# Last expert and final norm of a mixer and mixture-of-experts encoder: four row tiles normed early, two shared between GpSimd and ScalarE, the last products and the expert's own rows by halves

## The chip, the cores and the metric

The kernel runs on one core of one Trainium2 chip. The metric is the device time of one execution in microseconds. The engines are TensorE (PE in the profile; PEld is its weight load), VectorE (DVE), ScalarE (ACT), GpSimd (POOL) and SyncE (SP), which here only issues DMAs.

## The reference, cut to what matters

One encoder layer on 1024 tokens of width 1024, all in float32: a norm, a mixer with two branches, a norm, a mixture of 16 experts in which every expert chooses 128 tokens, and a final norm. The change lies wholly behind the mixer.

```python
# capacity = 2 * 1024 // 16 = 128 tokens for each expert
xg = h[idx]                                       # (16, 128, 1024)
act = silu(xg @ w_gate[e]) * (xg @ w_up[e])       # (128, 2816)
y = (act @ w_down[e]) * gate[e]                   # (128, 1024)
x = x + scatter_add(y, idx)
out = x * rsqrt(mean(x * x, axis=-1) + 1e-6) * norm_final
```

## The kernel before, in words

The function `experts` runs the 16 experts one after the other. `loop` makes a loop of 15 experts and writes the last one out by itself (`last` is true in its body). Each engine has its own instruction list, in a fixed order, and semaphores join them.

**Units.** An expert's weights come in 36 units, numbered k from 0 to 35 (`order`): gate and up products of a tile of 1024, 1024 or 768 hidden columns in four units each (units 0 to 15 and 20 to 27), and down products of the three tiles (units 16 to 19, 28 to 31, 32 to 35). A unit is two blocks of 128 rows; the last two, 34 and 35, have one block each. Float32 precision comes from two parts of each operand: the high part is a rounded copy and the low part the rest, and a product is three matmuls (high by high, high by low, low by high), so that a unit of two blocks is 12 matmuls of 512 (or 384) columns.

**What a unit goes through.** SP loads it into one of nine `raw` buffers as soon as the unit nine before it is split (L1884). ACT makes the high part (`split_high`, L1982), three units ahead of the product and not before the product of the unit four earlier is done, since there are four `part` buffers. DVE makes the low part (`split_low`, L2068), and PE multiplies (L2271 for gate and up, L2245 for down). Between them ACT computes Silu (L2020), DVE the product with `up` (L2132), PE transposes it (L2221), and ACT and DVE split the transposed tile (L2025, L2138). The program lists of ACT and DVE go by steps p from 0 to 35. In step p stand first the Silu, product or transpose work that falls due and then the split of unit k = p + 3, and behind it what `SQUARE_AT`, `MEAN_AT`, `SQRT_AT`, `ROOT_AT` and `NORM_AT` put at that k. The transpose of the third hidden tile stands ahead of unit 30 on PE (`TURN_AT`), its DVE part in step 31, ahead of the splits of units 34 and 35, and unit 32 needs it.

**The end.** The final norm works on eight tiles of 128 tokens. `x_mid` in HBM holds all rows but for what the last expert adds. Tiles 0 and 1 are loaded by POOL during the last expert into `store` and `early_sb`, squared by ACT with a sum for each row (`square_rows`, L2005), and their inverse root comes from DVE and ACT together: `mean_of_rows` (L2111), a square root on ACT (`root`, L2011) and five small operations on DVE (`inverse_root`, L93 to L97). `norm_row` (L2122) multiplies by the root and the gain row, and POOL stores the tile. Tiles 2 to 7 are loaded by SP, two tiles at a time, into raw buffers that have become free (L1900); their squares and norms stand behind the last split on ACT and DVE, and SP stores each behind its norm (L1909). ACT's square root needs another table than Silu, and `act_idle` (L2040) loads it ahead of the end.

The last expert's own rows are not scattered. POOL gathers them from `x_mid` into `xg`, and DVE adds the weighted products (L2178); they are squared, normed (L2186), and written over their rows of the output by an indirect DMA of POOL (L1968). This DMA waits for all stores of the eight tiles (`out_stored`, `early_stored`) and for `own_normed`, since the tiles' stores write stale versions of the same rows. In the order of DVE behind the loop: root and norm of tiles 2 and 3, mean and root of tiles 4 and 5, own rows added, norm of 4 and 5, mean and root of tiles 6, 7 and the own rows together, norm of 6 and 7, norm of the own rows.

The lines that the change touches and the prediction names: `order` and `TURN_AT` (L1758), the tables at L1805 to L1813, SP's loads and stores (L1900, L1909), POOL's part (L1938 to L1968), `square_rows` and `root` (L1997 to L2011), DVE's list behind the loop (L2169 to L2187), and PE's loop over `order` (L2224).

## Time and profile before

| | us |
|---|---|
| median of 3 runs | 2780.15 |
| lowest and highest run | 2779.88, 2780.17 |
| span of the profiled execution, from first to last instruction | 2777.4 |
| PE busy in the span | 2700.3 |
| DVE busy in the span | 1914.0 |
| ACT busy in the span | 1619.2 |
| POOL busy in the span | 221.1 |

The profiled execution has no time of its own beside its span; the median of the runs is 2.75 us above that span, which is what lies around it. Times in the rows are in microseconds from the start of the span, durations marked ns in nanoseconds. In a timeline, a group's first number is its start, the second its length, and brackets tell how long the engine had been idle and who released it. L12 is line 12 of the kernel before. Instructions of DVE and ACT overlap their neighbours by 0.08 to 0.1 us in the records, so a row of DVE costs its list some 0.08 less than its duration. In a group of several instructions the length is that of the whole group.

### The profile page before, as it was taken

The numbers are of one execution on the slowest core, as the hardware profiler recorded it, in microseconds if no ns is written. First come the engines' busy times: TensorE is split into PE (matmuls) and PEld (weight loads), VectorE is DVE, ScalarE is ACT, GpSimd is POOL, SyncE is SP. The second block draws the span as 40 slices with busy tenths as digits, with TensorE's granted clock in tenths as the row PEclk, the third lists the DMA queues.
The fourth block names the chain that finished last, engine by engine and source line by source line (L and its number), as shares of the span: only waits on it lengthen the run. The fifth ranks groups of instructions, "written<-read, shape, count | busy, mean of one in ns | idle before, by whom it ended". The sixth has DMA issues, their size and how long they took to land.

```text
span 2777.4 us, 36831 instructions
## 1 busy us (share of the span) xinstructions
PE 2700.3 (97%) x13530; PEld 2323.1 (84%) x13530; DVE 1914.0 (69%) x1928; ACT 1619.2 (58%) x1483; POOL 221.1 (8%) x242
## 2 busy tenths in 40 slices
PE   8999999999999999948999999999999999999997
PEld 7888888888888888847888888888888888888886
DVE  6624425364554234368889888988888888888887
ACT  6233334353442322326877787777777777877786
POOL 0011010100111111000000000000000000000010
PEclk9999999999999999979999999999999999999998
DMA  4133342421525433358999999999999999999997
GB/s 124 44 104 62 76 89 60 88 76 54 107 56 127 97 93 121 122 220 304 384 381 376 384 383 383 373 387 380 382 379 389 374 386 373 392 373 382 376 392 285
DMA packets 253891, 689.96 MB, mean 248 GB/s; under 512 B 18444, under 2 KB 75916, under 8 KB 253808
## 3 DMA queue, kind: packets, MB, share of 16 engines
q1 hardware_dynamic: 227968, 622.01, 59.9%
q0 software_dynamic: 25840, 66.80, 10.8%
q8 instruction: 58, 0.95, 0.1%
q14 instruction: 25, 0.20, 0.0%
HBM read 634.22 MB, written 54.53 MB: 248 GB/s over the span
## 4 chain that ended last, share of the span: by engine, by line
PE 53%; DVE 2%; issue 0%; DMA 0%; ACT 0%; DVEq 0%; POOL 0%; POOLq 0%; ACTq 0%
PE e_gate_ps L2271 17%; PE e_up_ps L2271 17%; PE e_y_ps L2245 17%; PE e_turn L2221 1%; PE e_turn L2205 1%; DVE e_part L2068 0%; DVE e_top_at L2084 0%; DVE e_top L2080 0%; DVE e_silu L2086 0%; DVE e_act L2086 0%; DMA e_xg<-h_mid,e_token_next 0%; DVE e_raw L2122 0%; DMA out_dram<-e_raw 0%; ACT e_part L1982 0%; DVE e_xg L2178 0%
## 5 line engine op out<-in xcount | busy, mean ns | idle before, releaser
L2068 DVE TENSOR_TENSOR e_part<-e_raw,e_part 128x2048 fp32r<-128x2048 f32 (+2 forms) x576 | 1196.5, 2111 | 176.2 <-ACT e_part L1982 172.9
L1982 ACT ACTIVATE e_part<-e_raw 128x2048 fp32r<-128x2048 f32 (+2 forms) x576 | 1008.7, 1773 | 307.8 <-PE e_y_ps L2245 167.9
L105 PE MATMUL m_proj<-m_hT,m_w_part 128*128 128x512 f32 (+1 forms) x2328 | 548.2, 393 | 1.8 <-ACT m_stage L622 1.8
L105 PEld LDWEIGHTS m_proj<-m_hT,m_w_part 128*128 128x128 f32 (+1 forms) x2328 | 434.3, 187 | 93.6 <-issue 2.2
L2245 PE MATMUL e_y_ps<-e_part,e_actT 128*128 128x512 f32 x2112 | 497.9, 392 | 0.4 <-DVE e_actT L2138 0.4
L2271 PE MATMUL e_gate_ps<-e_part,e_xgT 128*128 128x512 f32 (+1 forms) x2304 | 495.2, 372 | 0.0
L2271 PE MATMUL e_up_ps<-e_part,e_xgT 128*128 128x512 f32 (+1 forms) x2304 | 489.0, 371 | 0.0
L2271 PEld LDWEIGHTS e_gate_ps<-e_part,e_xgT 128*128 128x128 f32 x2304 | 421.9, 188 | 60.8 <-issue 0.3
L2271 PEld LDWEIGHTS e_up_ps<-e_part,e_xgT 128*128 128x128 f32 x2304 | 421.6, 188 | 59.9
L2245 PEld LDWEIGHTS e_y_ps<-e_part,e_actT 128*128 128x128 f32 x2112 | 392.6, 188 | 80.1 <-issue 0.8
L888 DVE TENSOR_TENSOR m_w_part<-m_w_raw,m_w_part 128x1024 fp32r<-128x1024 f32 (+1 forms) x93 | 112.7, 1218 | 142.1 <-ACT m_w_part L546 142.1
L105 PE MATMUL m_out<-m_w_part,m_hT 128*128 128x256 f32 x1536 | 192.5, 283 | 0.0
L105 PEld LDWEIGHTS m_out<-m_w_part,m_hT 128*128 128x128 f32 x1536 | 189.5, 191 | 3.0
L631 ACT ACTIVATE m_lit<-m_proj 128x512 f32<-128x512 f32 x64 | 38.3, 599 | 256.2 <-PE m_proj L105 256.2
L105 PE MATMUL m_proj<-m_oT,m_w_part 128*128 128x512 f32 x768 | 187.3, 394 | 0.2
L105 PEld LDWEIGHTS m_proj<-m_oT,m_w_part 128*128 128x128 f32 x768 | 140.6, 188 | 30.3 <-DVE m_w_part L888 1.6
L622 ACT ACTIVATE m_stage<-m_proj 128x512 f32<-128x512 f32 x128 | 75.9, 597 | 100.7 <-PE m_proj L105 100.7
L1920 POOL TENSOR_TENSOR e_pool_idle<-cst 128x1 f32<-128x1 f32 x30 | 26.3, 876 | 1316.6 <-ACT e_y L2056 1056.2
L546 ACT ACTIVATE m_w_part<-m_w_raw 128x1024 fp32r<-128x1024 f32 (+1 forms) x93 | 96.6, 1051 | 30.6 <-PE m_out L105 12.3
L105 PE MATMUL m_out<-m_w_part,m_mT 128*128 128x512 f32 x384 | 92.1, 394 | 1.8 <-DVE m_w_part L888 1.8
L105 PEld LDWEIGHTS m_out<-m_w_part,m_mT 128*128 128x128 f32 x384 | 70.7, 188 | 17.0 <-DVE m_w_part L888 2.7
L613 ACT ACTIVATE m_v<-m_out 128x512 f32<-128x512 f32 x32 | 19.1, 598 | 110.4 <-PE m_out L105 110.4
(289 smaller groups left out, 1848.4 us busy)
## 6 DMA issues: line engine op xcount, KB each, us to landing
e_raw<-in_w_down_dram SPq DMA_DIRECT2D x160, 1024.0 KB, 7.6
e_raw<-in_w_gate_dram SPq DMA_DIRECT2D x128, 1024.0 KB, 7.3
e_raw<-in_w_up_dram SPq DMA_DIRECT2D x128, 1024.0 KB, 8.6
e_raw<-in_w_gate_dram SPq DMA_DIRECT2D x64, 768.0 KB, 8.8
e_raw<-in_w_up_dram SPq DMA_DIRECT2D x64, 768.0 KB, 5.9
m_w_raw<-in_w_in_dram SPq DMA_DIRECT2D x64, 512.0 KB, 4.5
ret_sum<-m_stage POOLq DMA_DIRECT2D x64, 256.0 KB, 4.7
gla_sum<-m_stage POOLq DMA_DIRECT2D x64, 256.0 KB, 4.7
```

The lines of the kernel that those rows point to most:

```text
L105: last = nc.tensor.matmul(out, x_at(x[xi], kc), w_at(w[wi], kc), start=start and kc == 0 and (xi, wi) == (0, 0), stop=stop and kc == chunk ...
L546: nc.scalar.activation(part_block(n, 0), raw_block(n), ACT.Copy).then_inc(w_high, 1)
L622: proj_took(nc.scalar.activation(stage[:, n % 4], proj_bank(u)[:], ACT.Copy), u)
L631: proj_took(nc.scalar.activation(lit_sb[:, n % 4], proj_bank(u)[:], ACT.Silu if u[0] == "C" else ACT.Sigmoid), u)
L888: nc.vector.tensor_tensor(part_block(n, 1), raw_block(n), part_block(n, 0), ALU.subtract).then_inc(w_split, 1)
L1920: nc.gpsimd.tensor_tensor(pool_idle[:, at:at + 1], cst[:, C_EPS:C_EPS + 1], cst[:, C_EPS:C_EPS + 1], ALU.add).then_inc(carried, 1)
L1982: nc.scalar.activation(part[k % PARTS][0][:, 0:size(k)], raw[k % RAW][:, 0:size(k)], ACT.Copy).then_inc(w_high, 1)
L2068: nc.vector.tensor_tensor(part[k % PARTS][1][:, 0:size(k)], raw[k % RAW][:, 0:size(k)], part[k % PARTS][0][:, 0:size(k)], ALU.subtract).th ...
L2205: last = nc.tensor.transpose(turn[u][:, c, :], xg[:, kc * P:(kc + 1) * P], ident)
L2221: last = nc.tensor.transpose(turn[g][:, c, :], act_sb[:, b * P:(b + 1) * P], ident)
L2245: ins = nc.tensor.matmul(y_ps[:, half, :], actT[i % 2][xi][:, c, :], w[wi][:, j * D + 512 * half:j * D + 512 * half + 512], start=(i, c, x ...
L2271: ins = nc.tensor.matmul(dst[:, half, 0:half_wide], xgT[xi][:, kc, :], w[wi][:, j * wide + half * half_wide:j * wide + (half + 1) * half_w ...
```

## The change

- **Early tiles.** There are three `early` buffers beside `store`, and so tiles 0 to 3 are normed within the last expert. POOL loads tiles 2 and 3 once unit 11 of the last expert is split. Their squares stand on ACT behind the high parts of units 26 and 27, their mean on DVE behind the low part of unit 28, the root on ACT behind unit 29's and on DVE behind unit 30's, and their norms on DVE behind units 32 and 33. POOL stores them. The idle square root (L2040) is gone. SP's list keeps two loads of two tiles (4 and 5, 6 and 7), which wait for units 27 and 28.
- **Squares of tiles 4 and 5** stand on ACT behind the high parts of units 34 and 35. Behind the last split, DVE's list is: mean and root of 4 and 5, norm of 4, mean and root of 6 and 7, left half of the own rows, norm of 5, right half of the own rows, and the own rows' norm.
- **Tiles 6 and 7** are multiplied by the gain row on GpSimd (SBUF to SBUF, 128x1024, into `store` and the first early buffer), behind POOL's stores of tiles 2 and 3; ACT multiplies by the root (`place_row`), and SP stores them last.
- **Last products.** Units 33, 34 and 35 are multiplied first for the left 512 output columns (12 matmuls), which raise `half_done`, and then for the right 512 (12 matmuls). All 24 matmuls are those of before, in another order.
- **Own rows by halves.** Each half is added and squared by itself. Their mean, root and the norm of the left half are on DVE; the right half is multiplied by the gain on DVE into `silu` and by the root on ACT. `own_normed` is raised twice, and POOL's indirect DMA waits for both.

```diff
-        early_sb = sb("early", [P, D])
...
-        X_RAW = [None] + [(UNITS - RAW + m) % RAW for m in range(NT // 2 - 1)]
...
-        early = [store, early_sb]
+        early = [store, *early_sb]
...
+        X_RAW = [None] * (EARLY // 2) + [(UNITS - RAW + m) % RAW for m in range((NT - EARLY) // 2)]
...
-        END_GROUPS = ((0, 2), (2, 4), (4, 6), (6, OWN + 1))
-        SQUARE_AT = {16: 0, 17: 1}
-        MEAN_AT, SQRT_AT, ROOT_AT = 18, 19, 20
-        NORM_AT = {21: 0, 23: 1}
+        GAINED = {6: early[0], 7: early[1]}
+        KEPT = len(GAINED)
+        END_GROUPS = ((0, 2), (2, 4), (4, 6), (6, NT))
+        SQUARE_AT = {16: 0, 17: 1, 26: 2, 27: 3, UNITS - 2: 4, UNITS - 1: 5}
+        MEAN_AT, SQRT_AT, ROOT_AT = {18: 0, 28: 1}, {19: 0, 29: 1}, {20: 0, 30: 1}
+        NORM_AT = {21: 0, 23: 1, 32: 2, 33: 3}
+        FINAL = UNITS - 3
...
-                    for m in range(1, NT // 2):
-                        sp.wait_ge(w_split, UNITS * LAST + UNITS - RAW + m)
+                    for m in range(EARLY // 2, NT // 2):
+                        sp.wait_ge(w_split, UNITS * LAST + UNITS - RAW + m - EARLY // 2 + 1)
...
-                                     ).then_inc(x_in[EARLY + m - 1], 16)
+                                     ).then_inc(x_in[EARLY // 2 + m], 16)
...
-                sp.wait_ge(normed, t + 1)
-                sp.dma_start(out[0, t * P:(t + 1) * P, :], x_tile(t)).then_inc(out_stored, 16)
+                if t in GAINED:
+                    sp.wait_ge(row_placed, t - min(GAINED) + 1)
+                    src = GAINED[t][:]
+                else:
+                    sp.wait_ge(normed, t + 1)
+                    src = x_tile(t)
+                sp.dma_start(out[0, t * P:(t + 1) * P, :], src).then_inc(out_stored, 16)
...
+                        if t == KEPT:
+                            pool.wait_ge(w_split, UNITS * LAST + 12)
...
-                        pool.dma_start(out[0, t * P:(t + 1) * P, :], x_tile(t)).then_inc(early_stored, 16)
+                        pool.dma_start(out[0, t * P:(t + 1) * P, :], x_tile(t)).then_inc(early_stored[t >= KEPT], 16)
+                    pool.wait_ge(gain_in, 16)
+                    pool.wait_ge(early_stored[0], 16 * KEPT)
+                    pool.wait_ge(x_in[EARLY // 2 + min(GAINED) // 2], 16)
+                    for t in GAINED:
+                        nc.gpsimd.tensor_tensor(GAINED[t][:], x_tile(t), gain_row[:], ALU.mult).then_inc(row_gained, 1)
...
-            pool.wait_ge(early_stored, 16 * EARLY)
+            pool.wait_ge(early_stored[0], 16 * KEPT)
+            pool.wait_ge(early_stored[1], 16 * (EARLY - KEPT))
...
-            pool.wait_ge(own_normed, 1)
+            pool.wait_ge(own_normed, 2)
...
-                    act.wait_ge(x_in[t if t < EARLY else EARLY + t // 2 - 1], 16)
-                else:
-                    act.wait_ge(own_added, 1)
+                    act.wait_ge(x_in[t if t < EARLY else EARLY // 2 + t // 2], 16)
...
-                nc.scalar.activation(squares[:], x_tile(t) if t < OWN else xg[:], ACT.Square, accum_out=stat[:, 0, t:t + 1]
+                nc.scalar.activation(squares[:], x_tile(t), ACT.Square, accum_out=stat[:, 0, t:t + 1]
...
+            def square_own(half):
+                act.wait_ge(own_added, half + 1)
+                act.wait_ge(squared, NT + half)
+                nc.scalar.activation(squares[:, 0:D // 2], xg[:, half * (D // 2):(half + 1) * (D // 2)], ACT.Square,
+                                     accum_out=stat[:, 4 * half, OWN:OWN + 1]).then_inc(squared, 1)
+            def place_row(t):
+                act.wait_ge(row_gained, t - min(GAINED) + 1)
+                act.wait_ge(end_rooted, 1)
+                nc.scalar.activation(GAINED[t][:], GAINED[t][:], ACT.Copy, scale=stat[:, 2, t:t + 1]
+                                     ).then_inc(row_placed, 1)
...
-                    if last and k == SQRT_AT:
-                        root(0)
-                    if last and k == UNITS - 2:
-                        nc.scalar.activation(act_idle[:], cst[:, C_EPS:C_EPS + 1], ACT.Sqrt)
+                    if last and k in SQRT_AT:
+                        root(SQRT_AT[k])
...
-                    square_rows(2)
-                    square_rows(3)
-                    root(1)
-                    square_rows(4)
-                    square_rows(5)
...
-                    for t in range(6, OWN + 1):
-                        square_rows(t)
+                    square_rows(6)
+                    square_rows(7)
...
+                    place_row(6)
+                    square_own(0)
+                    place_row(7)
+                    square_own(1)
+                    act.wait_ge(meaned, len(END_GROUPS) + 1)
+                    nc.scalar.activation(stat[:, 1, OWN:OWN + 1], stat[:, 3, OWN:OWN + 1], ACT.Sqrt).then_inc(rooted, 1)
+                    act.wait_ge(own_gained, 1)
+                    act.wait_ge(end_rooted, 2)
+                    nc.scalar.activation(xg[:, D // 2:D], silu[:, 0:D // 2], ACT.Copy, scale=stat[:, 2, OWN:OWN + 1]
+                                         ).then_inc(own_normed, 1)
...
-                    if last and k == MEAN_AT:
-                        mean_of_rows(0)
-                    if last and k == ROOT_AT:
-                        root_of_rows(0)
+                    if last and k in MEAN_AT:
+                        mean_of_rows(MEAN_AT[k])
+                    if last and k in ROOT_AT:
+                        root_of_rows(ROOT_AT[k])
...
-            mean_of_rows(1)
-            root_of_rows(1)
-            norm_row(2)
-            norm_row(3)
+            def add_own(half):
+                at = slice(half * (D // 2), (half + 1) * (D // 2))
+                nc.vector.scalar_tensor_tensor(out=xg[:, at], in0=y_ps[:, half, :], scalar=weight[:, LAST:LAST + 1],
+                                               in1=xg[:, at], op0=ALU.mult, op1=ALU.add).then_inc(own_added, 1)
...
-            dve.wait_ge(gathered, 16 * EXPERTS + 16)
-            dve.wait_ge(unit_done, PARTS + UNITS * EXPERTS)
-            halves = xg[:].rearrange("p (h n) -> p h n", h=2)
-            nc.vector.scalar_tensor_tensor(out=halves, in0=y_ps[:], scalar=weight[:, LAST:LAST + 1], in1=halves,
-                                           op0=ALU.mult, op1=ALU.add).then_inc(own_added, 1)
...
-            norm_row(5)
...
-            norm_row(6)
-            norm_row(7)
-            nc.vector.scalar_tensor_tensor(out=xg[:], in0=xg[:], scalar=stat[:, 2, OWN:OWN + 1], in1=gain_row[:],
-                                           op0=ALU.mult, op1=ALU.mult).then_inc(own_normed, 1)
+            dve.sem_inc(end_rooted, 1)
+            dve.wait_ge(gathered, 16 * EXPERTS + 16)
+            dve.wait_ge(half_done, 1)
+            add_own(0)
+            norm_row(5)
+            dve.wait_ge(unit_done, PARTS + UNITS * EXPERTS)
+            add_own(1)
+            dve.wait_ge(own_added, 2)
+            nc.vector.tensor_tensor(silu[:, 0:D // 2], xg[:, D // 2:D], gain_row[:, D // 2:D], ALU.mult
+                                    ).then_inc(own_gained, 1)
+            own = lambda r: stat[:, r, OWN:OWN + 1]
+            dve.wait_ge(squared, NT + 1)
+            chain.link(nc.vector.tensor_scalar(own(2), own(0), 1.0 / D, EPS, ALU.mult, ALU.add))
+            dve.wait_ge(squared, NT + 2)
+            nc.vector.scalar_tensor_tensor(out=own(3), in0=own(4), scalar=1.0 / D, in1=own(2), op0=ALU.mult, op1=ALU.add
+                                           ).then_inc(meaned, 1)
+            dve.wait_ge(rooted, len(END_GROUPS) + 1)
+            inverse_root(nc, chain, own(2), own(1), own(3), own(4))
+            dve.sem_inc(end_rooted, 1)
+            nc.vector.scalar_tensor_tensor(out=xg[:, 0:D // 2], in0=xg[:, 0:D // 2], scalar=own(2),
+                                           in1=gain_row[:, 0:D // 2], op0=ALU.mult, op1=ALU.mult
+                                           ).then_inc(own_normed, 1)
...
+            def finish(e):
+                for half in range(2):
+                    for k in range(FINAL, UNITS):
+                        _, i, c0, n = order[k]
+                        pe.wait_ge(w_split, UNITS * e + k + 1)
+                        for j in range(n):
+                            c = c0 + j
+                            for xi, wi in ((0, 0), (0, 1), (1, 0)):
+                                ins = nc.tensor.matmul(
+                                    y_ps[:, half, :], actT[i % 2][xi][:, c, :],
+                                    part[k % PARTS][wi][:, j * D + 512 * half:j * D + 512 * half + 512],
+                                    start=False, stop=(c, xi, wi) == (BLOCKS[TILES - 1] - 1, 1, 0))
+                    if half:
+                        ins.then_inc(unit_done, UNITS - FINAL)
+                    else:
+                        ins.then_inc(half_done, 1)
...
+                    if last and k == FINAL:
+                        finish(e)
+                        break
```

## Rows read from the trace of the kernel before

**Rows 1.** First part of the page: busy time, share of the span and instructions.

```profile
PE 2700.3 (97%) x13530; PEld 2323.1 (84%) x13530; DVE 1914.0 (69%) x1928; ACT 1619.2 (58%) x1483; POOL 221.1 (8%) x242
```

**Rows 2.** The chain that ended last, its end; start us, us, what.

```profile
2750.88 8.44 PE e_y_ps L2245 x36
...
2759.44 1.28 DVE e_xg L2178
...
2766.98 2.71 DMA out_dram<-e_raw
...
2770.49 1.01 POOL out_dram L1968
```

**Rows 3.** Timeline of PE, units 32 to 35; brackets: idle before, and releaser.

```profile
2750.88 8.43 PE L2245 MATMUL e_y_ps<-e_part,e_actT 128*128 128x512 f32 x36 [0.42 <-DVE e_actT L2138]
```

**Rows 4.** Timeline of DVE, from the split of unit 27 on.

```profile
2733.83 8.50 DVE L2068 TENSOR_TENSOR e_part<-e_raw,e_part 128x1536 fp32r<-128x1536 f32 x4 [1.74 <-ACT e_part L1982]
2742.24 0.95 DVE L2132 TENSOR_TENSOR e_act<-e_silu,e_up_ps 128x768 f32<-128x768 f32 x1
2743.11 6.69 DVE L2068 TENSOR_TENSOR e_part<-e_raw,e_part 128x2048 fp32r<-128x2048 f32 x3
2749.72 1.01 DVE L2138 TENSOR_TENSOR e_actT<-e_turn,e_actT 128x512 fp32r<-128x512 f32 x2
2750.65 2.35 DVE L2068 TENSOR_TENSOR e_part<-e_raw,e_part 128x1024 fp32r<-128x1024 f32 x2
...
2754.37 0.17 DVE L93 RECIPROCAL e_stat<-e_stat 128x2 f32<-128x2 f32 x1 [0.27 <-ACT e_stat L2011]
...
2755.37 2.48 DVE L2122 SCALAR_TENSOR_TENSOR e_raw<-e_raw,e_stat,e_y 128x1024 f32<-128x1024 f32 x2
```

**Rows 5.** Timeline of ACT, from the split of unit 26 on.

```profile
2728.80 1.49 ACT L1982 ACTIVATE e_part<-e_raw 128x1536 fp32r<-128x1536 f32 x1 [0.87 <-PE e_gate_ps L2271]
2730.31 1.28 ACT L2020 ACT_TABLE_LOAD   x1
...
2732.31 8.70 ACT L1982 ACTIVATE e_part<-e_raw 128x1536 fp32r<-128x1536 f32 x5
```

**Rows 6.** Groups by form, 2700 to 2777 us; name, count | busy us, mean ns | idle.

```profile
L2138 DVE TENSOR_TENSOR e_actT<-e_turn,e_actT 128x512 fp32r<-128x512 f32 x3 | 2.0, 682 | 0.0
...
L2005 ACT ACTIVATE e_squares<-e_raw 128x1024 f32<-128x1024 f32 x6 | 6.3, 1056 | 0.3
```

**Rows 7.** GpSimd's only multiplications or additions among the experts, by source line.

```profile
L1920 POOL TENSOR_TENSOR e_pool_idle<-cst x30: 188/876/1562, 1284.8 to 2668.2; 128x1 f32<-128x1 f32 x30
```

**Rows 8.** Timeline around the last of these additions, of DVE and POOL.

```profile
2667.44 2.29 DVE L2068 TENSOR_TENSOR e_part<-e_raw,e_part 128x2048 fp32r<-128x2048 f32 x1
2668.22 1.56 POOL L1920 TENSOR_TENSOR e_pool_idle<-cst 128x1 f32<-128x1 f32 x1 [70.41 <-ACT e_y L2056]
```

**Rows 9.** Stretches: PE busy us (x instructions), granted clock, DMA share, GB/s.

```profile
947.00:950.00 3.00, 1.22 (x6) 1.00 0.00 0
...
2758.80:2762.20 3.40, 0.50 (x3) 1.00 0.39 155
2762.20:2765.00 2.80, 0.00 (x0) 0.50 0.81 326
```

**Rows 10.** Stretches at the experts' start: PE, PEld, DVE, ACT, POOL, clock, DMA, GB/s.

```profile
1261.00:1263.60 2.60, 2.60 (x8) 1.95 (x7) 2.36 (x3) 2.31 (x4) 0.00 (x0) 0.50 0.92 345
1264.00:1266.60 2.60, 2.60 (x13) 2.11 (x13) 2.26 (x2) 2.32 (x2) 0.00 (x0) 1.00 0.92 331
```

**Rows 11.** DMA queue of SP, 2757.5 to 2760.2 (two stores): packets, MB, share.

```profile
q1 hardware_dynamic: 283, 1.05, 96.7%
```

**Rows 12.** Load of unit 17: SP's issue, us to landing, and ACT's use of it.

```profile
2684.26 0.37 SPq L1884 DMA_DIRECT2D e_raw<-in_w_down_dram  x1
...
e_raw<-in_w_down_dram SPq DMA_DIRECT2D x1, 1024.0 KB, 16.9
...
2705.19 1.90 ACT L1982 ACTIVATE e_part<-e_raw 128x2048 fp32r<-128x2048 f32 x1
```

More of the change, by code:

```diff
@@ L1793, in experts @@
         stat = sb("stat", [P, 5, NT + 1])
-        early_sb = sb("early", [P, D])
+        early_sb = [sb(f"early{t}", [P, D]) for t in range(3)]
         squares = sb("squares", [P, D])
@@ L1848, in experts @@
         normed = sem("normed")
-        early_stored = sem("early_stored")
+        early_stored = [sem(f"early_stored{k}") for k in range(2)]
         out_stored = sem("out_stored")
         own_added = sem("own_added")
+        end_rooted = sem("end_rooted")
+        half_done = sem("half_done")
+        row_gained = sem("row_gained")
+        row_placed = sem("row_placed")
+        own_gained = sem("own_gained")
         own_normed = sem("own_normed")
```

2 lines of the change are left out of this document (1 added, 1 removed).

## The prediction

> **What bounds the kernel now.** I read the page first [rows 1]: PE is busy for 97% of the span, so a change of the end can give back only what lies behind the last product, and costs whatever it makes PE wait. The chain of waits comes next [rows 2]. The last product ends at 2750.88 + 8.44 = 2759.32. Behind it DVE adds the own rows and norms four tiles with a root between, the last store starts at 2766.98 and lands at 2769.69, and only then GpSimd issues the own rows' DMA. From landing to the span's end are 2777.4 - 2769.7 = 7.7 us, which the change leaves as they are. The end is thus 10.4 us of work on the tail plus 7.7.
>
> Then the timelines of the last expert. PE waits once in this stretch, 0.42 us ahead of unit 32, for DVE's part of the transposed tile [rows 3]. DVE waits 1.74 us for ACT ahead of unit 27's split and is then without a pause: four splits, the product with `up`, three splits, the transposed tile, two splits [rows 4]. In that stretch DVE sets PE's pace. ACT has no pause either from the split of unit 26 to that of unit 31: a table load, the Silu and five splits [rows 5]. The reader is to see that what is put on ACT between units 26 and 28, or on DVE between units 27 and 33, moves PE's last 36 matmuls one for one.
>
> **Part 1: early norms of tiles 2 and 3.** Their squares stand on ACT behind the splits of units 26 and 27. A square is 1.06 us [rows 6] and there are two, so the split of unit 27 comes 1.0 us later and that of 28 2.1 us later; DVE takes each at once when ACT is done, so it is 2.1 us late from unit 28 on. The mean adds 0.1. The square root stands on ACT behind unit 29; it brings its table load of 1.28 us (what the load ahead of the Silu costs in [rows 5]), and ACT reaches unit 30 so that DVE waits another 0.5. The root on DVE behind unit 30 is five operations in 1.0 us (from 2754.37 to 2755.37 in [rows 4]), and two norms behind units 32 and 33 are 2.48 for the pair [rows 4], say 2.4. The sum is 2.1 + 0.1 + 0.5 + 1.0 + 2.4 = 6.1 us. The cover is nothing: in the kernel before the transposed tile ends at 2750.73 [rows 4] and PE already waits for it. PE's last 36 matmuls start at 2757.0 and end at 2765.4. PE's stop ahead of unit 32 grows to some 3.8 us: the product with `up` ends on DVE at 2747.0, six transposes (0.6) and 24 matmuls at 0.23 (8.43 / 36, [rows 3]) end at 2753.2. The rest of the 6.1 is stops ahead of unit 28 and the transposes.
>
> The early loads and stores move 1 MB forward. The load with the least to spare is unit 17's: it lands at 2684.26 + 16.9 = 2701.2 and ACT takes it at 2705.19 [rows 12], 4.0 us later. SP's queue moved 1.05 MB in 2.7 us at 96.7% busy [rows 11], so two tiles more put it 2.6 us back and 1.4 are left. I take nothing. SP's loads of tiles 4 to 7 wait for the splits of units 27 and 28, as the first two of its three did, so they start as early as before. POOL issues two loads and two stores more, and waits first for unit 11's split; nothing else is queued there until the end.
>
> **Part 2: the tail with everything else hidden.** DVE ends the last split at 2753.0 + 6.1 = 2759.1. Behind it stand mean and root of 4 and 5 (0.1, a wait of 0.27 for ACT, 1.0), norm 4 (1.2), mean and root of 6 and 7 (1.4): 2763.1. The left half of the products is done 12 matmuls before the end, at 2762.7, so DVE adds it at once: a half is 0.7 (128x512 takes 0.68, [rows 6]), 2763.8. Norm 5 ends at 2765.0. The right half waits for PE (2765.4) and ends at 2766.2. From there the own rows need their square on ACT (0.7), mean (0.2), root with its wait (0.4 + 1.0) and the left norm (0.7): 2769.4. The stores of tiles 5, 6 and 7 all start about 2765 to 2766. One alone lands in 2.71 [rows 2], and two of them keep the queue 97% busy at 1.3 us each [rows 11], so the third lands 2.7 + 2 x 1.3 = 5.3 behind the first's start: 2770.3. This is what ends last. The span is 2770.3 + 7.7 = 2778.0. Tail saved, 18.1 - 12.6 = 5.5 us; part 1 has spent 6.1.
>
> Reordering the last 24 matmuls costs nothing: each has its own weight load before and after (13530 of both, [rows 1]). The tile multiplication on ACT (twice 1.06) stands between the root of 6 and 7 and the own rows' squares and is hidden behind the products' second half; without that cover it would be 1.0.
>
> **Part 3: GpSimd's multiplications.** They stand behind the norm of tile 3 and two DMA issues and so start near 2756.6, when DVE has units 34 and 35, two norms and the roots ahead of it. All those read two inputs from SBUF. The trace has GpSimd with 128x1 alone, 188 to 1562 ns [rows 7]. The long ones all look like the one shown: GpSimd starts at 2668.22 in the middle of DVE's split and ends at 2669.78, 0.05 us behind the split's end at 2669.73 [rows 8]; 15 of the 30 are such, with 1.56 us, and the others, beside DVE's small copies, take 0.19. So GpSimd doesn't work beside a DVE instruction with two inputs in SBUF. That DVE stands still in turn while GpSimd multiplies no row shows, but one thing at a time is the plain reading. The Trainium skill states it: SBUF - State Buffer, "Who interferes with whom", says that a DVE instruction with two SBUF inputs and a GpSimd instruction that reads SBUF lock each other out for the whole instruction. It speaks against this change; by it the case below holds rather than its rival.
>
> The size of a multiplication is unknown: 1.28 us is what DVE takes for the like (2.48 for two, less overlap), 2.56 would be one pass for each input. I take the middle, 1.9. Two of them are 3.8; DVE's own two waits for ACT's root (0.27 each) take 0.5 of it, leaving 3.3. DVE then reaches the left half at 2766.4, norm 5 ends at 2768.3, the last store lands at 2773.6. The span is 2781.3, the time 2781.3 + 2.75 = 2784.0. With 1.28 each it is 2782.8, with 2.56 each 2785.3. The Trainium skill, GPSIMD Engine Reference, "Performance versus the Vector engine", has 4497 ns for 2048 elements; half of it, 2.25 each, would give 2784.7 as an estimate.
>
> **Rivals.**
> - *GpSimd's multiplications are hidden.* DVE isn't held, and part 2 stands: 2778.0 + 2.75 = 2780.7. For it: no row shows DVE waiting for GpSimd. Against: GpSimd waits for DVE fifteen times of fifteen.
> - *Slower: TensorE's clock.* PE's stop of 3.8 us ahead of unit 32 is new. The granted clock fell from 1.00 to 0.50 at 2762.2, when PE had stood still 2.9 us, and did not with six matmuls in the 3 us from 947.0 [rows 9]. At the experts' start, PE did 8 matmuls in 2.6 us at 0.50 and 13 at 1.00 [rows 10], that is 1.2 against 2.4 GHz. If all 36 ran at the low level they would take 2 x 8.4, and PE would end at 2773.7. The own rows are done 4.0 us behind PE (2769.4 - 2765.4), so 2777.7, which gives a span of 2785.4 and a time of 2788.2. It decides only from the point where PE ends later than 2769.6, 4.2 us late or more than 18 of 36 matmuls at the low level; DVE's lateness of part 3 hides less than that. At the experts' start the level was back 2.5 us behind the first such product [rows 10], which would cost 1.3, hidden. So I think of a fall as likely and of this price as unlikely.
> - *Faster: PE's stops don't come.* If ACT and DVE took the early norms in pauses, and GpSimd were hidden, it would be 2780.7 - 6.1 = 2774.6. [rows 4] and [rows 5] speak against it: no pauses.
> - *The early loads hold the weights up.* With 1.4 us to spare at unit 17, it would need twice the DMA time that I gave the two tiles, and would then cost 1.2 on top.
>
> **How the numbers follow.** The chances are 0.60 for part 3 as told (2784.0; its own range with half a us on part 1 is 2782.3 to 2785.8), 0.23 for hidden multiplications (2780.7), 0.10 for the clock (2788.2, or less if it is partly back), 0.05 for the faster case and 0.02 for the loads. The range is 2778.0 to 2787.5; it leaves out the faster case, the clock's full price and the outermost of the costs. A measurement of this kernel can tell about 0.2%, or 5.6 us, from no change: the bounds are 2774.6 and 2785.7. Faster has the faster case, 0.05. Slower has the clock, 0.10, the upper edge of part 3, 0.07, and 0.02: 0.19. Between them lies 0.76.
>
> **What would show it.** Part 1: on PE's timeline stops ahead of unit 28, of the last transposes and of unit 32, together some 6 us, and the last product's end near 2765.4. Part 2: the gap between the last product and the end of the span shrinks from 18.1 to 12.6 with hidden multiplications and to some 15.9 with part 3. Part 3: DVE splits or norms that are as long as a GpSimd multiplication overlaps them, or pauses there; in the rival all splits of 34 and 35 keep 1.2 us. Clock: a stretch at 0.50 among the last 36 matmuls. I am wrong if a multiplication of GpSimd is over 2.8 us, or if ACT's squares find room that I don't see.

## The result, and the profile after

| | before | after |
|---|---|---|
| time, median (range) | 2780.15 us (2778.65 to 2781.57) | 2786.56 us (2784.57 to 2787.68) |
| span of the profiled execution | 2777.4 us | 2782.6 us (time 2785.08) |
| from ACT's split of unit 20 to the span's end | 63.58 us | 69.57 us |
| mean granted clock of the profiled execution | 0.986 | 0.987 |

The changed kernel is slower by 0.22%: the ratio is 1.0022, with a 95% interval of 1.0014 to 1.0030, or +6.4 us in the medians. The time was forecast at 2784.0. The measured one lies in the forecast's range (2778.0 to 2787.5) and 0.9 us beyond 2785.7, the bound of "slower", which had a chance of 0.19. The profiled execution after is one of the fastest of its kernel, and it comes to the last expert 0.79 us earlier than the one before; so I compare from ACT's split of unit 20 (2713.82 before, 2713.03 after), which gives +6.0 us. To lay a time of after beside one of before, add 0.79. Most of the rest of the +6.4 lies around the span: an execution's time is 2.46 us longer than its span after, and 2.14 before (medians of the executions of after, and of those of before beside the experiments). The 2.75 that the forecast added was the distance from a profiled span of 2777.4, a short one, to a median; before's median span is some 2778.0. Medians here and below leave out one execution, of experiment 10, that took 7282.56 us.

The page's first line answers [rows 1]:

```profile
PE 2701.3 (97%) x13530; PEld 2324.0 (84%) x13530; DVE 1917.6 (69%) x1935; ACT 1621.2 (58%) x1488; POOL 227.3 (8%) x248
```

No product is added, and GpSimd has 6.2 us more, most of it the two multiplications. PE's timeline from unit 28 on (units 28 to 31, six transposes, unit 32, the last three units by halves) answers [rows 3]:

```profile
2739.25 5.72 PE L2313 MATMUL e_y_ps<-e_part,e_actT 128*128 128x512 f32 x24 [1.01 <-DVE e_part L2102]
...
2746.24 0.88 PE L2268 MATMUL e_turn<-cst,e_act 128*128 128x128 f32 x6 [1.27 <-DVE e_act L2166]
...
2756.26 4.37 PE L2313 MATMUL e_y_ps<-e_part,e_actT 128*128 128x512 f32 x12 [3.67 <-DVE e_actT L2172]
2760.43 6.32 PE L2280 MATMUL e_y_ps<-e_part,e_actT 128*128 128x512 f32 x24
```

The three brackets are the stops that the forecast named: 1.01, 1.27 and 3.67 us, all for DVE, together 6.0. The last 24 products have no stop that the timeline shows, and the last ends at 2766.75, on before's clock 2767.54, which is 8.2 us later than before. DVE's timeline answers [rows 4]; its first two brackets below stand behind the squares of tiles 2 and 3, the third behind the square root:

```profile
2734.07 1.76 DVE L2102 TENSOR_TENSOR e_part<-e_raw,e_part 128x1536 fp32r<-128x1536 f32 x1 [2.77 <-ACT e_part L2003]
2736.90 2.29 DVE L2102 TENSOR_TENSOR e_part<-e_raw,e_part 128x2048 fp32r<-128x2048 f32 x1 [1.08 <-ACT e_part L2003]
...
2742.03 2.29 DVE L2102 TENSOR_TENSOR e_part<-e_raw,e_part 128x2048 fp32r<-128x2048 f32 x1 [0.57 <-ACT e_part L2003]
...
2756.03 6.95 DVE L2102 TENSOR_TENSOR e_part<-e_raw,e_part 128x1024 fp32r<-128x1024 f32 x2
...
2767.23 0.75 DVE L2205 SCALAR_TENSOR_TENSOR e_xg<-e_y_ps,e_weight,e_xg 128x512 f32<-128x512 f32 x1 [0.21 <-DVE e_stat L97]
```

The pauses are 1.03, 1.08 and 0.57 us longer than before. The two splits of units 34 and 35 took 6.95 us, where before they took 2.35 [rows 4]: DVE was held for 4.6 us. The reason is on the timeline of POOL (GpSimd):

```profile
2756.02 2.40 POOL L1965 TENSOR_TENSOR store<-e_raw,e_y 128x1024 f32<-128x1024 f32 x1
2758.37 2.38 POOL L1965 TENSOR_TENSOR e_early<-e_raw,e_y 128x1024 f32<-128x1024 f32 x1
```

They stand end to end, from 2756.02 to 2760.75, and the split of unit 34 runs beside both, from 2756.03 to 2761.84. The left half of the own rows is then added at 2767.23 straight behind DVE's own root (0.21, the usual step), so at the end it is DVE's list that is late, and not PE. Stretches of the window view answer [rows 9]; the columns are PE busy (instructions), granted clock, DMA share and GB/s:

```profile
2757.50:2760.90 3.40, 3.40 (x10) 0.50 0.10 41
2760.90:2767.00 6.10, 5.74 (x24) 1.00 0.09 37
```

Behind the stop of 3.67 us the granted clock was 0.50, that is 1.2 GHz, for 3.4 us, and then 1.00 again. The chain of waits ends so, and answers [rows 2]:

```profile
2756.11 6.86 DVE e_part L2102 x2
...
2768.93 1.05 ACT e_early L2036
2769.98 0.05 SPq L1922
2770.07 4.37 DMA out_dram<-e_early
2775.35 1.02 POOL out_dram L1989
```

The held splits stand in it; PE doesn't, from there on. ACT's placing of tile 7 (L2036) stands in it too, but without it the last store would hardly have started sooner: SP was issuing the store of tile 6 until 2770.02 (2769.59 + 0.43). The last store lands at 2774.44, 5.2 us behind the first start of the three (2769.20), and the span ends 8.2 us later.

### The profile page after: what moved, and what is told of

Its sections match the earlier page's. It is cut to its first block, busy times and chain, and to the rows that moved or that the text cites. A ratio compares the mean times of both kernels' runs of the same rounds, so it can differ in the third digit from the quotient of the medians.

```text
span 2782.6 us, 36855 instructions
## 1 busy us (share of the span) xinstructions
PE 2701.3 (97%) x13530; PEld 2324.0 (84%) x13530; DVE 1917.6 (69%) x1935; ACT 1621.2 (58%) x1488; POOL 227.3 (8%) x248
## 4 chain that ended last, share of the span: by engine, by line
PE 53%; DVE 2%; ACT 0%; DMA 0%; issue 0%; POOL 0%; POOLq 0%; ACTq 0%; DVEq 0%; SPq 0%
PE e_gate_ps L2339 17%; PE e_up_ps L2339 17%; PE e_y_ps L2313 17%; PE e_turn L2268 1%; DVE e_part L2102 1%; PE e_turn L2252 1%; DVE e_top_at L2118 0%; DVE e_top L2114 0%; ACT e_part L2003 0%; DVE e_silu L2120 0%; DVE e_act L2120 0%; DMA out_dram<-e_early 0%; DMA e_xg<-h_mid,e_token_next 0%; DVE e_early L2156 0%; DVE e_raw L2156 0%
```

## The experiments

Each run's expectation was written before it ran. "Split 34" is DVE's split of unit 34, 1.2 us by itself. The kernel before had a median of 2780.18 beside runs 1 to 4, 2780.14 beside 5 to 8 and 2779.94 beside 9 to 11.

**1. Without the multiplications.** ACT scales tiles 6 and 7 straight from their raw buffer, so their gain is left out.

```diff
-                    for t in GAINED:
-                        nc.gpsimd.tensor_tensor(GAINED[t][:], x_tile(t), gain_row[:], ALU.mult).then_inc(row_gained, 1)
+                    pool.sem_inc(row_gained, 2)
...
-                nc.scalar.activation(GAINED[t][:], GAINED[t][:], ACT.Copy, scale=stat[:, 2, t:t + 1]
+                nc.scalar.activation(GAINED[t][:], x_tile(t), ACT.Copy, scale=stat[:, 2, t:t + 1]
```

> The changed kernel without GpSimd's two multiplications: ScalarE scales tiles 6 and 7 straight from their raw buffer, so the gain is left out of these two tiles. Theory A (from unit 28 on VectorE's list sets the end, and GpSimd's two multiplications of 2.40 us hold it for 4.6 us): the split of unit 34 falls from 5.82 to 1.2 us, the last product stays at about 7 to 8 us behind that of the kernel before, and now the last product sets the end again: the own rows are done 4.0 us behind it. Span 3.7 us shorter than the changed kernel's, time about 2782.9, still above the kernel before. Theory B (TensorE's lateness sets the end and the multiplications lie beside it): the split gets shorter all the same, but the time moves by less than 1 us, to about 2786.

Measured: 2784.43 us (ratio 1.0012, 1.0003 to 1.0021), 2.1 less than after. DVE's two splits, its adding of the left half, PE's last 36 products, and the clock (with PE's products; two stretches):

```profile
2758.09 2.35 DVE L2101 TENSOR_TENSOR e_part<-e_raw,e_part 128x1024 fp32r<-128x1024 f32 x2
...
2766.91 0.75 DVE L2204 SCALAR_TENSOR_TENSOR e_xg<-e_y_ps,e_weight,e_xg 128x512 f32<-128x512 f32 x1 [2.43 <-PE e_y_ps L2279]
...
2758.32 5.46 PE L2312 MATMUL e_y_ps<-e_part,e_actT 128*128 128x512 f32 x12 [3.69 <-DVE e_actT L2171]
2763.58 5.94 PE L2279 MATMUL e_y_ps<-e_part,e_actT 128*128 128x512 f32 x24
...
2757.40:2764.20 6.80, 5.88 (x14) 0.50 0.23 94
2764.40:2769.60 5.20, 5.12 (x23) 1.00 0.16 64
```

The splits are back at 2.35, so the multiplications held them. But the low clock now lasted 6.8 us, PE took 11.2 us for its last 36 products (10.5 in after, 8.4 before), and DVE waited 2.43 us for the left half. The bound changed hands: 4.6 us were taken away, 2.1 came back. The mechanism was right; my price for it as a single step was too high.

**2. The norms of tiles 2 and 3 behind the last split.** Multiplications kept.

```diff
-        SQUARE_AT = {16: 0, 17: 1, 26: 2, 27: 3, UNITS - 2: 4, UNITS - 1: 5}
+        SQUARE_AT = {16: (0,), 17: (1,), UNITS - 2: (2, 3), UNITS - 1: (4, 5)}
-        NORM_AT = {21: 0, 23: 1, 32: 2, 33: 3}
+        NORM_AT = {21: 0, 23: 1}
...
+            mean_of_rows(1)
+            root_of_rows(1)
+            norm_row(2)
+            norm_row(3)
             mean_of_rows(2)
```

> The changed kernel with the squares, mean, root and norms of tiles 2 and 3 taken out from among units 26 to 33: squares on ScalarE ahead of those of tiles 4 and 5, the rest on VectorE behind the last split. All else as changed, GpSimd's multiplications too. Both theories: TensorE has no stop ahead of unit 32 over 0.5 us, no stretch at clock 0.50 among its last 36 matmuls, and the last product ends within 0.5 us of that of the kernel before. Theory A (VectorE's list sets the end): only the pauses of VectorE go that ScalarE's squares and root made it take (2.1 + 0.5 us), so the time is 2 to 3.5 us less than the changed kernel's, about 2783.5. Theory B (TensorE's lateness sets the end): all of it comes back, about 7 us, time about 2779.5.

Measured: 2786.67 us (1.0024, 1.0015 to 1.0034), the same as after. PE's only stop was the old 0.42, its last product ended at 2759.72, and the granted clock stayed 1.00 up to there. DVE's and POOL's timelines say why that brought nothing:

```profile
2756.37 0.17 DVE L93 RECIPROCAL e_stat<-e_stat 128x2 f32<-128x2 f32 x1 [2.50 <-ACT e_stat L2042]
...
2760.40 4.97 DVE L94 TENSOR_TENSOR e_stat<-e_stat 128x2 f32<-128x2 f32 x1
...
2760.69 2.36 POOL L1965 TENSOR_TENSOR store<-e_raw,e_y 128x1024 f32<-128x1024 f32 x1
```

DVE's pause for squares, table load and root moved from before the last split to behind it (2.50 us), and the multiplications met not a split but an operation on 128x2 numbers, which took 4.97 us instead of 0.16. My expectation missed since I had counted the pause as gone. PE's being 8 us late is thus not in itself what makes the changed kernel slow: the sum of DVE's list is.

**3. Four early tiles with one root, nothing on GpSimd, tiles 6 and 7 normed by DVE.**

```diff
-        END_GROUPS = ((0, 2), (2, 4), (4, 6), (6, NT))
-        SQUARE_AT = {16: 0, 17: 1, 26: 2, 27: 3, UNITS - 2: 4, UNITS - 1: 5}
-        NORM_AT = {21: 0, 23: 1, 32: 2, 33: 3}
+        END_GROUPS = ((0, EARLY), (EARLY, NT))
+        SQUARE_AT = {16: 0, 17: 1, 18: 2, 19: 3, UNITS - 2: 4, UNITS - 1: 5}
+        NORM_AT = {23: 0, 24: 1, 25: 2, 26: 3}
```

> A version built on theory A: four early tiles as changed, but squared at units 16 to 19, with one mean, one square root (unit 21) and one inverse root (unit 22) for all four, and normed behind units 23 to 26, ahead of the pause that VectorE has before unit 27. Tiles 6 and 7 are normed on VectorE, nothing on GpSimd; tiles 4 to 7 share one root; halves as changed. Theory A: the last product is less than 1 us later than in the kernel before, VectorE's list behind it is norm 7, own rows and their root, the last store lands 4.5 to 5.5 us behind the last product, span 2772 to 2773.5, time 2775 to 2776.5: about 0.17% faster than the kernel before. If early norms cost the full 1.2 us each wherever they stand (no pause takes them), the last product is 2.4 us late and the time about 2777.5.

Measured: 2778.02 us (0.9994, 0.9985 to 1.0003), above what I expected. DVE stood twice behind the last split:

```profile
2756.11 0.17 DVE L2123 TENSOR_SCALAR e_stat<-e_stat 128x4 f32<-128x4 f32 x1 [1.59 <-ACT e_squares L2011]
...
2757.62 0.18 DVE L93 RECIPROCAL e_stat<-e_stat 128x4 f32<-128x4 f32 x1 [1.35 <-ACT e_stat L2023]
```

The mean of four tiles waits for four squares (1.59), and the root then brings its table load (1.35), since no load stands ahead of it. That is 2.9 us, of which a better order might give some back.

**4. GpSimd beside DVE in the kernel before, in two forms.** One execution; a scratch tile is written and not used.

```diff
+                        if k == 26:
+                            nc.gpsimd.tensor_tensor(scratch[:], gain_row[:], gain_row[:], ALU.mult).then_inc(probed, 1)
+                            pool.wait_ge(probed, 1)
+                        else:
+                            nc.gpsimd.tensor_scalar(scratch[:], gain_row[:], 2.0, None, ALU.mult).then_inc(probed, 1)
```

> The kernel before with two more GpSimd instructions in the last expert, on a scratch buffer that nobody reads: a tensor_tensor 128x1024 (two inputs from SBUF) let go when ScalarE has split unit 26, and a tensor_scalar 128x1024 (one input from SBUF) when it has split unit 30. Theory A (a GpSimd instruction that reads SBUF and a VectorE one with two SBUF inputs exclude each other): the VectorE split beside the tensor_tensor takes its 1.75 us plus about 2.4, and a split beside the tensor_scalar, 2.28 us alone, is also lengthened, by the whole length of the tensor_scalar; the tensor_scalar may itself wait for the split under way. Rival: only the two-input form collides (the one-input form leaves the splits at 2.28 us).

Measured: 2779.4 us, span 2777.3.

```profile
2729.30 3.40 POOL L1952 TENSOR_TENSOR e_scratch<-e_y 128x1024 f32<-128x1024 f32 x1 [2.71 <-ACT e_part L1993]
...
2738.24 3.39 POOL L1955 TENSOR_SCALAR e_scratch<-e_y 128x1024 f32<-128x1024 f32 x1 [5.55 <-ACT e_part L1993]
2738.90 3.13 DVE L2079 TENSOR_TENSOR e_part<-e_raw,e_part 128x2048 fp32r<-128x2048 f32 x1
```

The first started within a DVE split, ended some 1.75 us behind that split's end, and lay in a pause of DVE: here GpSimd was second and waited, and DVE lost nothing, so this half didn't test whether DVE is held. The second, with one input, also started within a split, 0.74 us before that split's end, and the next split, 2.3 us by itself, took 3.13. This form collides too, but DVE lost only 0.85 us beside it. How much of the 3.39 is GpSimd's own waiting isn't told. It is one execution of each.

**5 and 6. Fifteen products without use ahead of unit 32,** which fill PE's stop; in 5 in the changed kernel, in 6 in the kernel of experiment 1.

```diff
+                    if last and k == begins["down", TILES - 1]:
+                        for _ in range(15):
+                            nc.tensor.matmul(gate_ps[:, 0, :], xgT[0][:, 0, :],
+                                             xgT[0][:, 0:4, :].rearrange("p c n -> p (c n)"), start=True, stop=True)
```

> The changed kernel with 15 more matmuls on TensorE (512 columns, into the gate bank that nobody reads any more), placed ahead of unit 32's wait, where TensorE stands still for 3.7 us: about 3.4 us of work. Nothing else is different. The granted clock then should not fall to 0.50 among the last 36 matmuls, and the last product ends about 1.4 us earlier than in the changed kernel (2.9 where the low stretch lasted 6.9 us). Theory A (with GpSimd's multiplications in place VectorE's list sets the end): the time stays within 1 us of the changed kernel's 2786.6. Theory B (the clock's fall sets part of the end): it gets 1.4 to 3 us shorter, 2783.6 to 2785.2.

> The same 15 matmuls in the version without GpSimd's multiplications (the gain left out of tiles 6 and 7). There VectorE waited 2.43 us for the left half of the products after a low stretch of 6.9 us. Theory C (once GpSimd is out of the way the clock's fall sets the end): no low stretch, VectorE's wait for the left half is under 0.5 us, the time falls by 1.5 to 2.9 us from 2784.4 to about 2782.2. Rival (the fall is a companion without effect): within 0.6 us of 2784.4.

Measured: 2786.59 us in 5 (1.0023, 1.0014 to 1.0032) and 2781.93 in 6 (1.0006, 0.9997 to 1.0015). Neither trace has a low stretch there. PE in 5, then DVE's two halves in 6:

```profile
2754.82 3.56 PE L2294 MATMUL e_gate_ps<-e_xgT 128*128 128x512 f32 x15
...
2764.32 0.96 PE L2280 MATMUL e_y_ps<-e_part,e_actT 128*128 128x512 f32 x3 [1.31 <-DVE e_part L2102]
```

```profile
2763.84 0.75 DVE L2204 SCALAR_TENSOR_TENSOR e_xg<-e_y_ps,e_weight,e_xg 128x512 f32<-128x512 f32 x1 [0.21 <-DVE e_stat L97]
...
2765.94 0.75 DVE L2204 SCALAR_TENSOR_TENSOR e_xg<-e_y_ps,e_weight,e_xg 128x512 f32<-128x512 f32 x1 [0.16 <-PE e_y_ps L2279]
```

In the changed kernel the faster clock brought nothing: PE only waited 1.31 us for the held split 34, and the last product, expected 1.4 us earlier, ended as far behind ACT's split of unit 20 as in after (53.8 against 53.7). With the multiplications out it brought 2.5 us, and DVE's waits for PE of 2.43 and 0.71 were gone. So the two costs lie beside each other: whichever is removed alone, the other remains: 2.1 us for the multiplications, nothing for the clock, 4.6 for both. Experiment 1's eleven times lie in two clusters, four from 2781.35 to 2782.01 and seven from 2783.98 to 2785.09; the lower is where experiment 6 is, which would fit executions with no long low stretch. The profile has only one execution, of the upper cluster, so this isn't shown.

**7. Experiment 3, mended:** one root for the early tiles and one more unit forward, tiles 4 and 5 apart from 6 and 7, the table load ahead of the root.

```diff
+        END_GROUPS = ((0, EARLY), (EARLY, NT - 2), (NT - 2, NT))
+        NORM_AT = {22: 0, 23: 1, 24: 2, 25: 3}
...
+                    if last and k == 32:
+                        nc.scalar.activation(act_idle[:], cst[:, C_EPS:C_EPS + 1], ACT.Sqrt)
```

> The one-root version with three edits: ScalarE loads the square root's table behind unit 32, where it is idle, instead of ahead of the last root; mean, square root and root of the four early tiles at units 19, 20 and 21 and the norms behind units 22 to 25, one unit earlier; tiles 4 and 5 have their own root again, so that VectorE doesn't wait for the squares of 6 and 7 (it stood 1.59 + 1.35 us there). Theory A: the last product ends up to 0.5 us earlier, norm 7 ends 1.3 us earlier, and the time is 1.3 to 2 us less than that version's 2778.0: about 2776.4, 0.13% under the kernel before. Rival (the tail was set by TensorE): no more than 0.5 us less.

Measured: 2776.86 us (0.9989, 0.9980 to 0.9998), 1.2 less than experiment 3, where 1.3 to 2 were expected. Counted from ACT's split of unit 20 (2714.90 here, 2713.60 in 3), norm 4 starts at 41.8 us and in experiment 3 at 45.0, so 3.2 earlier; the root that tiles 6 and 7 now have for themselves takes 1.4 back.

PE's timeline:

```profile
2736.46 4.43 PE L2321 MATMUL e_up_ps<-e_part,e_xgT 128*128 128x384 f32 x24 [0.49 <-DVE e_part L2083]
...
2753.23 3.00 PE L2295 MATMUL e_y_ps<-e_part,e_actT 128*128 128x512 f32 x12 [0.70 <-DVE e_actT L2153]
```

PE stops 1.2 us in all, not 6.0. Four early tiles can thus pay, with their chain where DVE has pauses, the table load where ACT has room, and nothing on GpSimd. What each of the three edits against experiment 3 is worth wasn't measured alone.

**8. The halves alone:** two early tiles as before, products and own rows by halves.

```diff
+        SQUARE_AT = {16: 0, 17: 1}
+        NORM_AT = {21: 0, 23: 1}
...
             add_own(0)
             dve.wait_ge(unit_done, PARTS + UNITS * EXPERTS)
             add_own(1)
             norm_row(4)
             norm_row(5)
```

> One part alone: the kernel before with the left half of the last 24 products first and the own rows added, squared, normed by halves as changed; two early tiles as before, tiles 2 to 7 normed on VectorE in the order of before, no multiplication on GpSimd. The last store now needs VectorE's list only up to norm 7: 0.75 for the right half behind the last product in place of 1.28, then norms 4, 5, root, 6, 7, and the own rows' own root (1.5) and half norms go beside the last store's landing. Theory A: 0.5 us shorter than the kernel before, 2779.6. Rival (the own rows' separate root and the extra small instructions outlast the store): equal or up to 0.6 us longer.

Measured: 2780.27 us (1.0002, 0.9993 to 1.0011); nothing, as the rival said. DVE's adding of the own rows in the kernel before; then, from this kernel, DVE's last operation and GpSimd's DMA behind it:

```profile
2759.44 1.28 DVE L2178 SCALAR_TENSOR_TENSOR e_xg<-e_y_ps,e_weight,e_xg 128x1024 f32<-128x1024 f32 x1 [0.29 <-PE e_y_ps L2245]
...
2769.56 0.75 DVE L2222 SCALAR_TENSOR_TENSOR e_xg<-e_xg,e_stat,e_y 128x512 f32<-128x512 f32 x1 [0.16 <-DVE e_stat L97]
...
2771.16 1.01 POOL L1975 DMA_INDIRECT out_dram<-e_xg,e_token_next  x1 [42.89 <-DVE e_xg L2222]
```

Here the own rows end last (2770.31), just behind the last store's landing (2770.08). With two early tiles DVE comes to the own rows when PE is all but done: before, it waited only 0.29 us for the last product. Behind ACT's split of unit 20 the norm of tile 7 ends at 53.0 us here and at 53.1 before, so the halves save 0.1 there, and the own rows' separate root ends after it.

**9. Experiment 7 with the last products in the old order,** both halves side by side.

```diff
-                for half in range(2):
-                    for k in range(FINAL, UNITS):
+                for k in range(FINAL, UNITS):
...
+                            for half in range(2):
```

> The second one-root version with the last 24 products in the order of the kernel before (both halves of the output columns for each block), everything else equal; the left half is then done with the last product and no longer 12 matmuls ahead of it. In the second one-root version VectorE took the left half at 2760.53, with the last product at 2761.68. Theory A (VectorE's list behind the last splits sets the end): VectorE now stands 1.2 to 1.3 us for the left half with nothing else to do, and the time is 1.2 us longer, about 2778.1. Rival (the order of the products is worth nothing, as the own rows' root and the stores end last anyway): within 0.3 us of 2776.9.

Measured: 2777.43 us (0.9992, 0.9983 to 1.0001), 0.6 over experiment 7; the intervals overlap, but nine of the eleven times lie above 2777.04, where three of experiment 7's do.

```profile
2759.96 0.75 DVE L2186 SCALAR_TENSOR_TENSOR e_xg<-e_y_ps,e_weight,e_xg 128x512 f32<-128x512 f32 x1 [1.08 <-PE e_y_ps L2262]
```

The wait of 1.08 us is the left half's, and from unit 20 to the end it is +1.06 in the traces. So the order of the products is worth 0.6 to 1.1 us here, where DVE gets to the own rows before PE is done; in experiment 8, where it doesn't, it was worth nothing.

**10. Experiment 7 with the stores of tiles 2 and 3 on SP's queue.**

```diff
-                    for t in range(EARLY):
+                    for t in range(KEPT):
                         pool.wait_ge(normed, t + 1)
...
-            for t in range(EARLY, NT):
+            for t in range(KEPT, NT):
                 sp.wait_ge(normed, t + 1)
```

> The second one-root version with tiles 2 and 3 stored by SP ahead of tile 4 instead of by GpSimd, so that GpSimd issues two DMAs fewer. The span's last item is a drain of GpSimd's sequencer: 3.17 us in the kernel before and in the version with the halves alone, 3.50 in the changed kernel and in all with four early tiles. Theory: it grows with GpSimd's DMA count, the loads included: 3.2 to 3.4 us here, time 0.1 to 0.3 us less than 2776.9. Rival (it depends on something else): 3.50 as before.

Measured: 2776.53 us (0.9987, 0.9978 to 0.9996), 0.3 under experiment 7, whose interval overlaps with its own. It has the lowest median of this study, 3.4 us under the kernel before and 10 under the changed one. GpSimd's last step, in which it drains its queue, took 3.33 us; it was 3.50 in experiment 7 and in the changed kernel (four loads and four stores on GpSimd) and 3.17 in the kernel before and in experiment 8 (two and two). The spans differ by 0.2 in their medians, which is what the shorter drain explains.

**11. The multiplications one by one:** the second waits for the last split.

```diff
                     for t in GAINED:
+                        if t == 7:
+                            pool.wait_ge(w_split, UNITS * EXPERTS)
```

> The changed kernel with GpSimd's second multiplication waiting for the last split, so that VectorE gets a turn between the two. Theory A (what counts is the sum of the time that VectorE is held): the split of unit 34 takes 1.2 + 2.4 = 3.5 us instead of 5.82, TensorE's stop for it gets 1 us or more shorter, and the second multiplication holds one of the operations of the root or the norm behind it for about 2.4 us: the time stays within 0.8 us of 2786.6. Theory B (what counts is the late split, through TensorE): 1.3 to 2.4 us less.

Measured: 2785.53 us (1.0021, 1.0012 to 1.0030), 1.0 under after, between the theories, and the intervals overlap, so it decides between neither.

```profile
2758.14 4.59 DVE L2104 TENSOR_TENSOR e_part<-e_raw,e_part 128x1024 fp32r<-128x1024 f32 x2
...
2763.28 1.95 DVE L94 TENSOR_TENSOR e_stat<-e_stat 128x2 f32<-128x2 f32 x1
```

Apart, they hold DVE for 2.24 and 1.79 us, 4.0 in all where back to back it was 4.6. They hold DVE where they stand, with a split or with a few numbers beside them.

## Why the prediction was right and wrong

**Part 1, the early norms: right.** Stops were forecast ahead of unit 28, of the transposes and of unit 32, some 6 us with 3.8 for the last; they were 1.01, 1.27 and 3.67. The transposed tile was to end 6.1 us late, at 2756.83, and did at 2756.11 + 0.79 = 2756.90. The squares made DVE wait 1.03 and 1.08 us and the root 0.57, against 1.0, 1.1 and 0.5. The last product was to end near 2765.4 and did at 2767.54; its 36 products took 10.5 us instead of 8.4, with the low clock among them; but experiment 5 shows that the held split 34 keeps PE as late without it. The loads' smallest margin was 1.4 us, as forecast, though at unit 19 and not at unit 17, which kept 2.8; that rival fell, and so did the faster case.

**Part 2, the tail: the order right, its end mis-sized.** Three stores landed 5.2 us behind the first start, against 5.3. "From landing to the span's end are 2777.4 - 2769.7 = 7.7 us, which the change leaves as they are" is the step that was off: it was 8.2 (0.45 more, unrounded). Of this, 0.33 is GpSimd's last step, its draining, with four DMAs more. From the last split to the adding of the left half DVE took 4.3 us by its list, against 4.0. With the multiplications out and the stop filled (experiment 6) the time was 2781.9, against 2780.7 for this part with hidden multiplications. Two sums of the forecast are slightly off, without weight for the time: the own rows' steps from 2766.2 add up to 2769.2 and not 2769.4, and twice 8.4 behind 2757.0 is 2773.8.

**Part 3, the multiplications: the mechanism right, two terms mis-sized.** DVE stands still while GpSimd multiplies: experiment 1 shows it for split 34, and experiments 2 and 11 for an operation on 128x2 numbers too. I put one at 1.9 us, the middle between 1.28 and 2.56; it was 2.40 and 2.38, nearer to one pass for each input. And I let DVE's waits for ACT's root cover 0.5; the two multiplications stood beside a split, the waits came later with their 0.27 each, and nothing was covered. Together, 3.3 us of lateness were forecast and DVE was held for 4.6, which is 1.3 us of the miss. In the Trainium skill, GPSIMD Engine Reference, "Performance versus the Vector engine", 4497 ns stand for 2048 elements; half of it, 2.25 us for 1024, is an estimate, and nearer to the trace's 2.40 than my 1.9. The Trainium skill's page SBUF - State Buffer, "Who interferes with whom", has the two block each other fully for a whole instruction; the held splits and the 4.97 us for 128x2 agree. That page of the Trainium skill also has the one that issues first take precedence; experiment 4's first half agrees, while in the changed kernel both started at 2756.02, and which one was granted first there isn't told by the records.

The sum: +3.9 forecast for the span, +6.0 measured. Of the 2.1, 1.3 is the multiplications (their length and the missing cover), 0.4 the end and 0.3 DVE's steps between the last split and the left half; 0.1 is left without a place. With the first two alone the same steps give 2785.7 to 2785.8, at the bound of "slower", and with the third they pass it. That the likeliest case named "no change" and the kernel came out slower is thus due to these sizes and not to the mechanism; that 2786.56 still lies in the range owes something to the range's width.

**The clock.** I called a fall likely and its full price unlikely. The fall came, over 3.4 us that 10 products touch, and cost the changed kernel nothing (experiment 5), since DVE was held meanwhile. But "DVE's lateness of part 3 hides less than that" took the two as rivals that exclude each other. They aren't: with the multiplications out the clock cost 2.5 us (1 against 6). Its price was also put on the wrong path. The forecast let it act only through the last product and the own rows behind it, from 18 products at the low level on; in experiment 1 the low stretch touches 14, and the price came through the left half, for which DVE waited 2.43 us ahead of norm 5 and the last three stores. The time of 2788.2 didn't come.

**The change as a whole.** Its parts are of different worth. The halves bring nothing by themselves (experiment 8) and 0.6 to 1.1 beside four early tiles (9). Four early tiles are good if their chain lies between units 16 and 25 with one root (7), and cost PE 6.0 us of stops where two of them are normed between 26 and 33. GpSimd's share held DVE for 4.0 to 4.8 us at each place tried, where DVE norms two tiles by itself in 2.48.

**What stays open.** Why the low stretch was 3.4 us in one kernel and 6.8 in another after stops of 3.67 and 3.69 us, and whether another form on GpSimd (one input, 0.85 held) could pay, which wasn't tried in place. The 1.5 us between the profiled execution of after and its median lie ahead of unit 20, as far as the traces tell: the profiled execution of experiment 5 is 2.4 us longer than that of after, comes to ACT's split of unit 20 2.4 us later (2715.42 against 2713.03), and has the same end behind it (69.6 us in both). Why executions differ there is open.

## What to carry to other kernels

In these runs a GpSimd multiplication with two inputs in SBUF held any DVE operation with two inputs in SBUF that stood beside it for nearly as long as GpSimd took, which was 1.9 times DVE's own time for the same multiplication, and an operation on 128x2 numbers waited as long as a split. Ask what DVE has to do meanwhile before you call such work free. Before moving norms ahead into a loop that runs without pauses, look for the stretch in which both engines of the chain have room, gather the tiles under one root, and load its table ahead of it. Where two costs lie beside each other, take both away in one experiment as well as each alone: the sum of the single gains (2.1 and 0 us here) is not the gain of both (4.6).

## What the runs showed of the hardware that I had not expected

- Two GpSimd multiplications back to back held one DVE instruction over both, 5.82 us for a split of 1.2 and 4.97 for 128x2 numbers that take 0.16.
- With a single input GpSimd's 128x1024 was recorded with 3.39 us, the first 0.74 beside a split already under way, and the next DVE split lost only 0.85 (one execution).
- GpSimd's draining at the end took 3.17, 3.33 and 3.50 us with four, six and eight DMAs of whole tiles on it.
- After stops of 3.7 us the granted clock was 0.50 for 3.4 us in one kernel and 6.8 in another, and it stayed 1.00 where the stop was filled (experiments 5 and 6).
